# Scaling the odd head's attention weights on GpSimd with a product of two tensors in place of a product with a scalar for each row

## The reference

```python
def hybrid_layer(h, ...):                     # twice
    z = rms_norm_2(h, norm_g) @ w_in
    # heads 0..7: forgetting attention, heads 8..15: dilated attention, each of 64 columns
    ...

def one_block(args):                          # forgetting attention, 128 queries at a time
    s = einsum(q_i, k) * scale
    s = s + c_i[..., :, None] - c[:, :, None, :]
    s = where(causal, s, NEG)
    prob = softmax(s, axis=-1)
    return einsum(prob, v)
...
```

## Time and profile before

| | |
|---|---|
| Median of 3 runs | 3245.6 us (3244.81 to 3246.3) |
| Profiled execution, its own time | 3239.4 us |
| Its span, first to last instruction | 3237.6 us |
| PE busy | 3195.7 us, 99% |
| DVE busy | 1682.2 us, 52% |
| ACT busy | 1373.3 us, 42% |
| POOL busy | 157.6 us, 5% |
| Granted TensorE clock, mean | 0.999 |

### The profile page before, as it was taken

The page is one execution under the profiler, slowest core; times in us unless marked ns, Lnnn a source line. Parts: engine busy times, 40 slices in busy tenths (PEclk is TensorE's granted clock), DMA queues, the critical chain, the costliest instruction groups (busy, mean ns, idle before and its releaser), DMA issues.

```text
span 3237.6 us, 39934 instructions
## 1 busy us (share of the span) xinstructions
PE 3195.7 (99%) x16990; PEld 2663.7 (82%) x16990; DVE 1682.2 (52%) x2281; ACT 1373.3 (42%) x1783; POOL 157.6 (5%) x192
## 2 busy tenths in 40 slices
PE   9999999999999999999999999999999998999999
PEld 8888887898788888888887798788888886788867
DVE  5443348754544433443347756444443558554674
ACT  5222248633432223222326744342223656554573
POOL 0000001100000000000001100000000004100050
PEclk9999999999999999999999999999999999999999
DMA  4222221022122222222321103122222221122202
GB/s 177 91 96 90 101 79 66 27 91 92 65 91 104 83 99 105 92 103 85 111 79 65 53 27 130 53 94 102 91 94 105 80 90 40 61 103 91 76 25 89
DMA packets 47472, 275.07 MB, mean 85 GB/s; under 512 B 5312, under 2 KB 8896, under 8 KB 22208
## 3 DMA queue, kind: packets, MB, share of 16 engines
q1 hardware_dynamic: 47296, 272.53, 23.6%
HBM read 270.41 MB, written 2.10 MB: 84 GB/s over the span
## 4 chain that ended last, share of the span: by engine, by line
PE 92%; DVE 4%; ACT 2%; issue 1%; POOL 0%; DMA 0%; DVEq 0%; SPq 0%; ACTq 0%
PE banks L329 80%; PE banks L1544 1%; PE banks L1737 1%; PE banks L1720 1%; PE banks L2392 1%; PE banks L2433 1%; PE banks L1580 1%; ACT weights L2769 1%; DVE weights L2813 1%; PE banks L1559 1%; PE banks L1744 1%; PE banks L1241 0%; PE banks L1529 0%; ACT slab_hi L311 0%; DVE slab_lo L318 0%
## 5 line engine op out<-in xcount | busy, mean ns | idle before, releaser
L329 PE MATMUL banks<-x_hi,slab_hi 128*128 128x512 f32 x2560 | 1007.0, 393 | 9.6 <-DVE dil_qk L1171 7.9
L329 PE MATMUL banks<-x_hi,slab_lo 128*128 128x512 f32 x2560 | 998.0, 390 | 0.0
L329 PE MATMUL banks<-x_lo,slab_hi 128*128 128x512 f32 x2560 | 997.4, 390 | 0.0
L311 ACT ACTIVATE slab_hi<-slab_raw 128x2048 fp32r<-128x2048 f32 (+2 forms) x274 | 479.9, 1751 | 926.3 <-PE banks L329 924.8
L318 DVE TENSOR_TENSOR slab_lo<-slab_raw,slab_hi 128x2048 fp32r<-128x2048 f32 (+2 forms) x274 | 572.6, 2090 | 409.0 <-ACT slab_hi L311 409.0
L329 PEld LDWEIGHTS banks<-x_hi,slab_hi 128*128 128x128 f32 x2560 | 481.5, 188 | 115.9 <-issue 14.2
L329 PEld LDWEIGHTS banks<-x_lo,slab_hi 128*128 128x128 f32 x2560 | 481.6, 188 | 101.4 <-issue 2.9
L329 PEld LDWEIGHTS banks<-x_hi,slab_lo 128*128 128x128 f32 x2560 | 481.2, 188 | 101.5
L329 PE MATMUL banks<-hidden_hi,slab_hi 128*128 128x512 f32 x704 | 273.9, 389 | 0.0
L329 PE MATMUL banks<-hidden_lo,slab_hi 128*128 128x512 f32 x704 | 273.9, 389 | 0.0
L329 PE MATMUL banks<-hidden_hi,slab_lo 128*128 128x512 f32 x704 | 273.9, 389 | 0.0
(11 more groups left out here) (384 smaller groups left out, 4294.8 us busy)
## 6 DMA issues: line engine op xcount, KB each, us to landing
slab_raw<-slabs SPq DMA_DIRECT2D x195, 1024.0 KB, 4.8
slab_raw<-slabs SPq DMA_DIRECT2D x64, 704.0 KB, 4.0
slab_raw<-slabs SPq DMA_DIRECT2D x16, 640.0 KB, 3.9
h<-xT SPq DMA_DIRECT2D x8, 256.0 KB, 5.3
memory<-memT SPq DMA_DIRECT2D x2, 1024.0 KB, 5.5
out<-h SPq DMA_DIRECT2D x7, 256.0 KB, 4.9
constants<-con SPq DMA_DIRECT2D x1, 1412.5 KB, 9.5
slab_raw<-slabs SPq DMA_DIRECT2D x4, 256.0 KB, 4.7
```

The costliest lines, as they stand in the source:

```text
L311: self.nc.scalar.activation(self.wh[:, g % self.HIGHS, 0:w], self.raw[:, g % self.RAWS, 0:w], ACT.Copy).then_inc(self.hi_ready, 1)
L329: mm = self.nc.tensor.matmul(out, left[a], right[c], start=start and n == 0, stop=stop and n == 2)
```

## The change

GpSimd's product for the odd head becomes a TENSOR_TENSOR: both inputs are tensors, and the second is the column of `row_scale` read again for each of the block's 128, 256, 384 or 512 elements (a broadcast access pattern with step zero, no copy). The output, the order of the instructions, their number (64, of them 32 in each stage), and every wait and signal stay.

```diff
@@ -2743,7 +2743,8 @@
             pool.wait_ge(*self.inv_ready.at(u + 1))
             for tb, at in self.blocks(u):
                 w = self.weights(u, 1)[:, at]
-                ins = self.k.nc.gpsimd.tensor_scalar(w, w, self.col(self.ri, tb, 1), None, ALU.mult)
+                r = self.col(self.ri, tb, 1).broadcast_to([P, (tb + 1) * P])
+                ins = self.k.nc.gpsimd.tensor_tensor(w, w, r, ALU.mult)
             ins.then_inc(self.p_b.sem, 1)
             if u % self.UNITS == 1 and u >= 2 * self.UNITS:
                 self.low(pool, u // self.UNITS - 2)
```

## The result

The changed kernel takes 3258.05 us (median of 6 runs, 3257.02 to 3259.11) against 3245.2 us (6 runs, 3241.14 to 3246.3) for the kernel before: a ratio of 1.0043, 95% interval 1.0033 to 1.0053. It is slower by 13 us, where 3242.9 was predicted, and outside the range. The first rival had 3257.

The account below looks back on a forecast made before the run. VectorE was taken as full in the middle attention pairs. Gains of 0.84 us (stalls) and 0.49 us (end) a layer, 2.7 us in both, took 3245.6 to 3242.9 us; range 3238.5 to 3248.0.

Parts of the forecast that it names:

- The first rival: Attention pairs: GpSimd gets the port before VectorE's products, 1.3 us a pair less 0.2 gained, 3257 us; chance 0.12.
- So the new form doesn't ask sooner: Argument against GpSimd getting the port first: new form reaches for it about 0.15 us after its start, old form 0.13.
- The stall behind x_lo: Middle pairs: VectorE's 512-column product waits for GpSimd's x_lo; 0.21 us less in four pairs, 0.84 us a layer.
- the forecast's own step: Middle pairs: x_lo ends 0.21 us sooner, so VectorE's 512-column product falls from 0.95 to 0.74 us and the pair shortens equally.
- the pair that the prediction counted at nothing: Each layer's 7.90 us pair, holding its first stall: VectorE has 0.56 us idle there, so no gain was counted.
- other wait: Rival in the attention pairs: the gain goes to another wait, only the end's 1.0 us is left, 3244.6 us; chance 0.05.
- The end: End of each attention stage, where TensorE waits for GpSimd: 384-column product loses 0.21 us, 512-column 0.28; 0.49 us a layer.
- Unit 0: GpSimd's 128-column product between VectorE's 128 and 256: taken as 0, bounds -0.11 and +0.25 us, four times a layer.
- Length: GpSimd's product in the new form: 1.28 us for 512 columns, saving 0.28; 1.03 us for 384, saving 0.21.
- the rival of the nearly free column: GpSimd's repeated column is not read anew: 0.78 us for 512 columns, 0.66 for 384; 3238.6 us; chance 0.08.
- The distance: Whole kernel: the median before, 3245.6 us, lies 6.2 us above the profiled execution, and nothing in the change alters that.

Follow-up runs that it names:

- The wait for p_a: Changed kernel with GpSimd waiting for VectorE's product of the same unit, not the reciprocal: 3239.54 us, ratio 0.9986; same wait in the kernel before: 3247.32 us.
- the first experiment: Changed kernel with a one-column memset on GpSimd between its wait and its product, some 0.1 us: 3238.69 us, ratio 0.9984 to the kernel before.

## Why the prediction was wrong

**What it had right.** VectorE is the fullest engine of a pair; the port is the link between the two engines; the new form is the shorter one, even by more than the 0.28 and 0.21 us (0.52 and 0.41: 1.56 to 1.04, 1.24 to 0.83). The first rival named what happened, its engine and its place. Its size, 3257 against 3258.05, is in part luck: it had 1.1 us net a pair where 1.51 was measured, because it left out the product over 512 columns (1.37 us in place of 0.95), and it left out what the ends gave back.

**The step that failed** is in that rival: "So the new form doesn't ask sooner." It compared 0.13 and 0.15 us, each worked out from how long a held-up instruction was held up, to judge a gap of hundredths. Those figures, differences of rounded durations, are good to some 0.02 us, and what decided was of that size: GpSimd's row begins 0.06 us behind VectorE's in the old form and 0.04 to 0.05 in the new one. How much of the new form's lead is in that and how much comes behind the start of its row isn't shown. Worse, only one side was looked at. A row's start is not the claim: with a constant in place of its scalars VectorE is first at the same gap. What the runs showed in that step's place: GpSimd comes first in nearly every unit, VectorE's 384 columns take 1.09 us and not 0.42, and a middle pair 8.90 and not 7.40. So the forecast's premise, that VectorE keeps its 0.42 us at 384 columns, stood on two figures too coarse to carry it, and 0.12 was too little for the rival. The rule that the prediction cites from the Trainium skill ("SBUF — State Buffer", "Who interferes with whom": whoever issues first holds the pair for the whole instruction) fits the two-input form, with stalls of 0.67 and 0.88 us behind products of 0.83 and 1.04.

**Terms of the sum.** *The stall behind x_lo* was sized 0.21 us a pair in four pairs, on the ground that VectorE is full and the chain goes through it. Taking away 0.40 to 0.46 us gave 0.08 us in a middle pair, and 0.35 and 0.1 to 0.2 in the first two. The wait for p_a tests the forecast's own step, since VectorE's 0.95 became 0.74 there: that gave 0.52 us a layer where 0.84 was forecast, and the largest part of it (0.21) came in the pair that the prediction counted at nothing. The "other wait" that had 0.05 is the true one: VectorE's 7.29 us of busy time held 0.46 of standing, and behind it stands the 7.31 us of the other waits. *The end* was sized 0.49 us a layer. Between profiles without a clock drop there it is 0.6 (11.01 to 10.40). Against three of the four profiles of the kernel before it is 2.0 (12.4 to 10.4), since the clock stayed up as well. That, and not the middle, is most of the 5 us that the first experiment wins: 2 x 2.0 from the ends, and 2 x 0.7 from the pairs (45.3 for the six from the second to the seventh, 46.0 before). *Unit 0* was taken at 0 with 0.25 as its bound. It lost 0.5 (1.17 against 0.66). Where GpSimd stays behind (the wait for p_a) it takes 0.55, the 0.11 that the prediction kept as the other bound. *Length*: the products came out at 1.04 and 0.83 us, between the forecast's 1.28 and 1.03 and the rival of the nearly free column, whose own lengths are misworked: 1.3 ns a column and the fixed 0.28 us make 0.95 and 0.78, not 0.78 and 0.66. *The distance* of 6.2 us between profiled execution and median was said to be untouched by the change; some 3 us of it were the two clock drops at the ends, which the changed kernel's profile doesn't have, and 1.1 to 2 us the longer ones at the stages' beginnings.

**The account of the 13 us.** From the first layer's second pair to the last, the changed kernel takes 54.3 us where the one before takes 46.0: 8.3 a layer. Its end is 10.46 against 12.4, 1.9 less. 2 x (8.3 - 1.9) = 12.8, and 12.85 were measured. That it fits to a tenth is luck: it sets one profile against the ends of three others and leaves out the two first pairs, 32.45 us together in the changed kernel and 31.5 to 32.4 in those three.

## What to carry to other kernels

Where VectorE and GpSimd are released by the same semaphore for products in SBUF, as here, hundredths of a microsecond can decide which holds the other up. Decide it yourself, by letting the less urgent one wait for the other's product, before judging a change of form. An engine's busy time can hold standing time, so subtract the stalls before calling it the bound, and ask what the next chain of waits takes. And look at more than one profile where the median lies above the profiled time: the difference may be clock drops that some executions have and others don't.

## What the runs showed of the hardware

- **How long a GpSimd product in front holds VectorE up depends on its form.** The stalls of VectorE over 384 and 512 columns are 0.84 and 1.11 us behind two full tensors, 0.67 and 0.88 behind a tensor and a repeated column, 0.32 and 0.43 behind the one-input form: 2.2, 1.7 and 0.84 ns a column. For the first two that is nearly the whole instruction (0.84 of 1.00 us and 0.67 of 0.83, at 384 columns). The third is a third of what the instruction takes for a column (2.5 ns), and VectorE ended well before it. The Trainium skill ("SBUF — State Buffer", "Who interferes with whom") has the port held for the whole instruction; for the one-input form these runs show otherwise. It isn't settled how: in the earlier trace rows the product of 2761.10, which came 1.0 us after the one-input product had begun, still ended behind it.
- **A repeated column is cheaper than a full second tensor**: 0.83 and 1.04 us for 384 and 512 columns (1.64 ns a column) against 1.00 and 1.27 (2.1 ns). The Trainium skill ("GPSIMD Engine Reference", section "Instruction dispatch") has about 2.5 cycles an element as the floor for two inputs; at its 1.2 GHz the full tensor agrees, and the column of step zero lies below, at 2.0.
- **The order can turn within one execution**: in the old form with a constant, 3 times one way and 13 the other, at rows 0.04 to 0.05 us apart. In the changed kernel the order turns at one place: in the first unit of the first layer's stage VectorE was first (0.69 us for its two products, 1.11 for GpSimd's), in the first unit of the second layer's stage GpSimd was (1.17 and 0.97). In both, GpSimd had been idle for over 190 us.
